# A two-layer hybrid mixer network: norms by token parts between three tiles on either side, and a folded Fourier mixer

## The chip, the cores and the metric

The kernel runs on one core of one Trainium2 chip. Its engines work at the same time and wait for one another by semaphores: TensorE (PE, matrix products), VectorE (DVE), ScalarE (ACT), GpSimd (POOL) and SyncE (SP, which only issues transfers). The metric is the device time of one execution in microseconds.

## What is computed

Two layers over 512 latent tokens and 256 context tokens, 1024 features each. Each layer normalises, modulates, projects to four groups of mixers, projects back and adds; then the same around a gated feed-forward network (FFN). From the reference, cut:

```python
u = modulate(rms_norm(x, g_pre_mix[l]), sh1, sc1) @ w_in[l]
...
o_b = fourier_mix(ub) @ w_fnet[l]      # real part of a 2-D FFT over tokens and 64 channels
...
mix = jnp.concatenate([merge(o_a), o_b, merge(o_c), o_d], axis=-1) @ w_out[l]
x = x + gt1 * rms_norm(mix, g_post_mix[l])
ffn = swiglu(modulate(rms_norm(x, g_pre_ffn[l]), sh2, sc2), w_ffn_in[l], w_ffn_out[l])
x = x + gt2 * rms_norm(ffn, g_post_ffn[l])
```

The context runs through the same weights in layer 0 with its own modulation. In layer 1 it is only needed for keys, values and states, so most of that layer works on the 512 latent tokens alone. `sh1`, `sc1`, `gt1` and their kind are products of the conditioning vectors with a large matrix.

## The kernel before

Features lie on the 128 partitions in 8 chunks (NC), tokens along the free dimension. The width T is 768 (TOK) in layer 0 and 512 (LAT) in layer 1. A weight tile has 128 output features and up to 8 chunks of contraction. Each is split into a high part (ScalarE, L570) and a low part (VectorE, L1154), the activations too, and one chunk takes three fp32r products: high by high, high by low, low by high (`passes`, L808). At T of 768 each is two products of 384 columns, in two PSUM banks; at 512 it is one. Tiles alternate between `ps[0]` and `ps[1]`.

The weights stream through three slots (RING = 3). SyncE loads tile k when tile k-3 has been multiplied:

```python
sp.wait_ge(blk_done, k - RING + 1)
sp.dma_start(raw[:, k % RING], wstream[tile_source(k)]).then_inc(raw_ld[k % RING], 16)
```

A layer is 22 projection tiles, the attention and recurrence mixers, the Fourier mixer, 8 output tiles ("wout"), and three FFN pieces of 8, 8 and 6 hidden chunks (`FFN_CHUNKS`), each with its "in" tiles and 8 "out" tiles.

Between two phases stands a norm. The post norm needs the squares of all 8 finished tiles: GpSimd squares and adds the first seven (L491, L493), ScalarE squares the last (L713), and TensorE sums over partitions with a matrix of ones in exact f32 (L871). ScalarE makes the inverse root by a logarithm and an exponential (L708, L709). VectorE then scales each chunk (L1248) and adds it to x (L1252). The pre norm squares the new x chunk by chunk (ScalarE L702, TensorE L859), makes a root, and produces the modulated input's high half (ScalarE L723) and low half (VectorE L1226, L1233). The next phase begins with two tiles side by side, which take each chunk as its low half is ready; a third tile's weights are loaded already.

The Fourier mixer multiplies channels with `fn_d` (L883), ScalarE copies (L778), then tokens are multiplied with cosine and sine tables of full width in exact f32 (L891), VectorE copies (L1514), and `fn_w` is applied (L899). The modulation columns of the coming stages are made by "pairs": GpSimd loads two rows (L477) when the reductions before them are done, and VectorE does four reductions over 1024 elements (`ada_pair`, L1166) that write their dump into `ps[3]`. In layer 0 pairs 8 and 9 stand in the Fourier mixer, 10 and 11 among the output tiles, the rest in the FFN.

Every engine takes its instructions in the order written.

## Time and profile before

| | |
|---|---|
| time, median of 3 runs | 1851.71 us (1851.44 to 1854.57) |
| the profiled execution's own time | 1851.98 us |
| its span | 1850.2 us |
| TensorE busy | 1704.0 us |
| VectorE busy | 980.6 us |
| ScalarE busy | 596.2 us |
| GpSimd busy | 149.1 us |
| mean granted TensorE clock | 0.974 of full |

The span runs from the first to the last instruction; the execution's own time has 1.8 us around it. Busy time says how much an engine worked, not whether the end waited for it: for that the profile has a chain, followed back from the last instruction to what released each step.

### The profile page before, as it was taken

The page shows a single profiled execution, that of the slowest core. Times are in us where ns is not written, and L with a number is a line of the kernel's source. Part 1 is how long each engine was busy: PE and PEld are TensorE (multiplying, and loading weights), DVE is VectorE, ACT ScalarE, POOL GpSimd, SP SyncE. Part 2 cuts the span into 40 slices and gives each one's busy share as a digit, 9 for nine tenths or more (in the row PEclk, how much of TensorE's full clock was granted, in tenths as well). Part 3 has the DMA queues.
Part 4 walks back from the last instruction along what each step waited for, and adds up shares of the span by engine and source line. Part 5 has one row for each costly group of instructions (what it writes and reads, how often), then busy time and mean ns, then how long its engine had stood idle before and what let it go on. Part 6 is the DMA issues. An engine that isn't in the chain of part 4 may idle for free.

```text
span 1850.2 us, 24632 instructions
## 1 busy us (share of the span) xinstructions
PE 1704.0 (92%) x10460; PEld 1501.7 (81%) x10460; DVE 980.6 (53%) x1603; ACT 596.2 (32%) x796; POOL 149.1 (8%) x186
## 2 busy tenths in 40 slices
PE   2699998999799999999999979898899899999996
PEld 1699987769599999999999959796667587887874
DVE  7987536865566544555554372653762632233334
ACT  2334433732332222221122143542462422332231
POOL 1010001004100000000000400000103000000003
PEclk9899999999899999999999989999999899999998
DMA  8261124132133334333432202113402132232222
GB/s 335 88 204 48 47 63 105 50 114 84 54 103 116 124 125 135 116 126 125 128 113 91 69 23 69 58 47 83 112 34 69 46 102 91 91 102 91 91 92 102
DMA packets 80638, 178.84 MB, mean 97 GB/s; under 512 B 38912, under 2 KB 39424, under 8 KB 80272
## 3 DMA queue, kind: packets, MB, share of 16 engines
q1 hardware_dynamic: 66864, 122.70, 21.7%
q0 software_dynamic: 13664, 54.56, 8.6%
q8 instruction: 83, 1.36, 0.3%
q14 instruction: 27, 0.22, 0.0%
HBM read 175.14 MB, written 2.10 MB: 96 GB/s over the span
## 4 chain that ended last, share of the span: by engine, by line
PE 85%; DVE 9%; DMA 3%; ACT 2%; issue 1%; SPq 0%; DVEq 0%; ACTq 0%
PE psum L808 73%; PE psum L969 2%; PE psum L980 2%; PE psum L1003 2%; DMA ada_0a<-in_adaT 1%; DVE f_t L1248 1%; PE psum L1034 1%; DVE x L1252 1%; PE psum L859 1%; DVE tmp L1226 1%; PE psum L891 1%; DVE psum L1545 1%; DVE w_lo L1154 1%; DVE psum L1166 1%; DVE s_sb L1324 1%
## 5 line engine op out<-in xcount | busy, mean ns | idle before, releaser
L808 PE MATMUL psum<-h_hi,w_hi 128*128 128x384 f32 (+1 forms) x1872 | 560.4, 359 | 32.1 <-DVE h_lo L1233 27.3
L808 PE MATMUL psum<-h_lo,w_hi 128*128 128x384 f32 (+1 forms) x1872 | 547.5, 352 | 0.0
L808 PE MATMUL psum<-h_hi,w_lo 128*128 128x384 f32 (+1 forms) x1872 | 547.2, 352 | 0.0
L1154 DVE TENSOR_TENSOR w_lo<-raw,w_hi 128x1024 fp32r<-128x1024 f32 x194 | 241.2, 1243 | 352.2 <-ACT w_hi L570 350.9
L808 PEld LDWEIGHTS psum<-h_hi,w_hi 128*128 128x128 f32 x1872 | 342.7, 190 | 61.5 <-issue 34.7
L570 ACT ACTIVATE w_hi<-raw 128x1024 fp32r<-128x1024 f32 x194 | 205.6, 1060 | 501.3 <-DMA raw<-in_wstream 501.2
L808 PEld LDWEIGHTS psum<-h_lo,w_hi 128*128 128x128 f32 x1872 | 346.4, 190 | 20.6 <-issue 1.7
L808 PEld LDWEIGHTS psum<-h_hi,w_lo 128*128 128x128 f32 x1872 | 345.6, 190 | 19.9
L1166 DVE CUSTOM_DVE_ANT_0 psum<-ada_w,c_b 128x1024 f32<-128x1024 f32 x160 | 202.2, 1264 | 16.3 <-issue 3.7
L1194 DVE TENSOR_TENSOR tmp<-tmp,psum 128x768 f32<-128x768 f32 (+1 forms) x44 | 36.1, 821 | 263.6 <-PE psum L808 263.6
L808 PE MATMUL psum<-hid_hi,w_hi 128*128 128x384 f32 (+1 forms) x528 | 160.2, 357 | 15.6 <-DVE w_lo L1154 13.2
L808 PE MATMUL psum<-hid_lo,w_hi 128*128 128x384 f32 (+1 forms) x528 | 159.1, 355 | 0.0
L808 PE MATMUL psum<-hid_hi,w_lo 128*128 128x384 f32 (+1 forms) x528 | 159.0, 355 | 0.0
L808 PEld LDWEIGHTS psum<-hid_hi,w_hi 128*128 128x128 f32 x528 | 97.0, 189 | 27.1 <-DVE w_lo L1154 17.3
L808 PEld LDWEIGHTS psum<-hid_hi,w_lo 128*128 128x128 f32 x528 | 97.7, 190 | 7.0
L808 PEld LDWEIGHTS psum<-hid_lo,w_hi 128*128 128x128 f32 x528 | 97.8, 190 | 6.7
L859 PE MATMUL psum<-sq,consts 128*128 128x512 f32 (+1 forms) x112 | 50.0, 604 | 51.8 <-ACT sq L702 51.7
L477 POOL DMA_DIRECT2D ada_w<-in_adaT x78 | 41.3, 530 | 635.7 <-DVE ada_t L1166 635.1
L859 PEld LDWEIGHTS psum<-sq,consts 128*128 128x128 f32 x112 | 23.8, 226 | 77.5 <-issue 50.2
L491 POOL TENSOR_TENSOR sq<-f_t 128x768 f32<-128x768 f32 (+1 forms) x28 | 41.1, 1467 | 537.5 <-DVE f_t L1181 446.6
L692 ACT ACTIVATE hid_hi<-tmp 128x768 fp32r<-128x768 f32 (+1 forms) x44 | 32.5, 739 | 116.8 <-DVE tmp L1194 116.8
L588 ACT ACTIVATE u_t<-psum 128x768 f32<-128x768 f32 (+1 forms) x44 | 33.6, 763 | 100.7 <-PE psum L808 100.4
(168 smaller groups left out, 1453.9 us busy)
## 6 DMA issues: line engine op xcount, KB each, us to landing
raw<-in_wstream SPq DMA_DIRECT2D x196, 512.0 KB, 3.6
ada_w<-in_adaT POOLq DMA_DIRECT2D x80, 512.0 KB, 4.0
ada_0a<-in_adaT SPq DMA_DIRECT2D x6, 1024.0 KB, 14.3
x<-in_xT POOLq DMA_DIRECT2D x4, 1536.0 KB, 10.9
na_r<-in_rpb SPq DMA_DIRECT2D x64, 64.0 KB, 3.4
fn_l<-in_dftL POOLq DMA_DIRECT2D x2, 2048.0 KB, 8.2
ada_0b<-in_adaT SPq DMA_DIRECT2D x2, 1024.0 KB, 19.3
out_xT<-x SPq DMA_DIRECT2D x4, 512.0 KB, 2.8
```

What stands on the lines that cost most here:

```text
L477: pool.dma_start(ada_w[:, u], adaT[2 * ADA_ORDER[q] + (2 * ADA_FIRST + u)]).then_inc(ada_ld[u], 16)
L491: link(pool.tensor_tensor(sq[:, 1 if b == 0 else 0, 0:T], f, f, ALU.mult))
L570: act.activation(w_hi[:, k % RING].rearrange("p c n -> p (c n)"), raw[:, k % RING], ACT.Copy)\
L588: act.activation(as_product(u_t[:, blk, 0:T], T), product_of(ps[b % 2], T), ACT.Silu if blk >= QD else ACT.Copy).then_inc(bank_free[b % 2], 1)
L808: mm = pe.matmul(ps[u][:, at:at + hi - lo], w[:, slot, k], r[:, k, lo:hi], start=first, stop=last)
L859: mm = pe.matmul(ps[2][:, lo:hi], ones, sq[:, c % 2, lo:hi], start=c == 0, stop=c == NC - 1)
L969: mm = pe.matmul(dst, q, keys, start=True, stop=True)
L980: mm = pe.transpose(pt_ps[:, n * j + P * c:n * j + P * c + P], s_sb[:, v % 3, j, o:o + P], ident)
L1003: mm = pe.matmul(dst, val, pt_sb[:, v % 2, n * j + P * c:n * j + P * c + P], start=c == 0, stop=c == n // P - 1, skip_group_check=True)
L1154: dve.tensor_tensor(w_lo[:, k % RING].rearrange("p c n -> p (c n)"), raw[:, k % RING], w_hi[:, k % RING].rearrange("p c n -> p (c n)").bit ...
L1166: dve.tensor_tensor_reduce(ps[3][:], ada_w[:, u], c_b[:, v], 1.0, 0.0, ALU.mult, ALU.add, ada_t[:, u, v:v + 1]).then_inc(ada_done, 1)
L1194: dve.tensor_tensor(as_product(tmp[:, 1, 0:T], T), as_product(tmp[:, 0, 0:T], T), product_of(ps[1], T), ALU.mult).then_inc(bank_free[1], 1)
```

## The change

1. **Norms by token parts.** The tokens are divided in two: in layer 0 the 256 context tokens (part 0) and the 512 latent ones (part 1), in layer 1 two halves of 256. The last three tiles before a norm (`tail`) are multiplied first for part 0 and then for part 1, and the first three tiles after it (`head`) as well. Each part has its own squares, roots, post and pre norm. TensorE's sums of squares of part 0's new x stand inside the second tail tile, those of part 1's post norm inside the first head tile. The head's part 1 takes all three tiles chunk by chunk; in layer 0's widths it is one product of 384 and one of 128 columns. The third tile of tail and head uses `ps[3]`. The last norm has no pre norm, and its stores go out by part.
2. **Fourier mixer folded.** A cosine table is symmetric and a sine table antisymmetric, so only n/2+1 cosine and n/2-1 sine columns are multiplied. ScalarE copies the sine sums, VectorE adds them to the cosines and subtracts them in reversed order for the other half. The tables are loaded in two transfers each.
3. **Modulation pairs.** In layer 0 pairs 8 and 9 leave the Fourier mixer: output tile pairs 0, 1 and 2 now have pairs (8, 9), 10 and 11. GpSimd loads 9, 10 and 11 each before two of its squares. The FFN's pairs shift by a tile. The third tail tile waits until pair 11 is copied.

```diff
+TAIL, HEAD = 3, 3
+def norm_parts(T):
+    return ((LAT, TOK, 1, 512), (0, LAT, 0, 0)) if T == TOK else ((0, T // 2, 0, 0), (T // 2, T, 0, 512))
...
+            def head_pieces(T, p):
+                if T == TOK:
+                    return ((0, HALF, 0), (HALF, LAT, 512)) if p else ((LAT, TOK, 512 + LAT - HALF),)
+                lo, hi, _, _ = norm_parts(T)[p]
+                return ((lo, hi, lo),)
+            def tail(g0, rhs_hi, rhs_lo, kc, T, nb, pre):
+                parts = norm_parts(T)
+                for p, (lo, hi, _, at0) in enumerate(parts):
+                    for j in range(TAIL):
+                        b = N_OUT - TAIL + j
+                        if p == 0:
+                            pe.wait_ge(w_lo_done, 2 * g0 + b + 1)
+                            if j < 2:
+                                pe.wait_ge(bank_free[b % 2], b // 2 + (g0 + 1))
+                            elif nb < 2:
+                                pe.wait_ge(ada_copied, (13, 41)[nb])
+                        else:
+                            pe.wait_ge(tail_free, TAIL * nb + j + 1)
+                        for k in range(kc):
+                            mm = passes_into(tail_bank(j), 2 * g0 + b, k, rhs_hi, rhs_lo, ((lo, hi, at0),), k == 0, k == kc - 1)
+                            if k == kc - 1:
+                                mm.then_inc(blk_done if p else tail_done, 1)
+                            if p and j == 0 and k == 2:
+                                late_mean_square(parts[0])
+                            if p and j == 1 and pre:
+                                part_mean_square(parts[0], NC * k // kc, NC * (k + 1) // kc)
+            def head(g0, T, nb):
...
+                for j in range(HEAD):
+                    pe.wait_ge(w_lo_done, 2 * g0 + j + 1)
+                    for k in range(NC):
+                        if j == 0:
+                            pe.wait_ge(hlo_ready, base + k + 1)
+                        passes_into(head_bank(j), 2 * g0 + j, k, h_hi, h_lo, head_pieces(T, 0), k == 0, k == NC - 1)
+                        if j == 0 and k == 3:
+                            late_mean_square(parts[1])
+                part_mean_square(parts[1], 0, NC)
+                for u in range(2):
+                    pe.wait_ge(bank_free[u], g0 + 1)
+                for k in range(NC):
+                    pe.wait_ge(hlo_ready, base + NC + k + 1)
+                    for j in range(HEAD):
+                        mm = passes_into(head_bank(j), 2 * g0 + j, k, h_hi, h_lo, head_pieces(T, 1), k == 0, k == NC - 1)
+                        if k == NC - 1:
+                            mm.then_inc(blk_done, 1)
```

The order on ScalarE and on VectorE in one norm (definitions of the steps left out; `copied` is ScalarE's copy of a wout tile, `added` VectorE's add of an FFN tile):

```diff
+                for j in range(TAIL):
+                    copied(0, j)
+                post_root(0)
+                pre_root(0)
+                copied(1, 0)
+                split_hi(2 * (g0 + N_OUT // 2))
+                normed_hi(0, 0, NC // 2)
+                copied(1, 1)
+                normed_hi(0, NC // 2, NC)
+                split_hi(2 * (g0 + N_OUT // 2) + 1)
+                copied(1, 2)
+                post_root(1)
+                split_hi(2 * (g0 + N_OUT // 2) + 2)
+                pre_root(1)
+                normed_hi(1, 0, NC)
...
+                for j in range(TAIL):
+                    added(0, j)
+                root()
+                post(0, 0, NC)
+                dve.wait_ge(x_upd, nx[0])
+                added(1, 0)
+                if pre is None:
+                    added(1, 1)
+                    added(1, 2)
+                    root()
+                    post(1, 0, NC)
+                    dve.wait_ge(x_upd, nx[0])
+                    return
+                root()
+                normed(0, 0, NC // 2)
+                split_lo(nxt)
+                added(1, 1)
+                normed(0, NC // 2, NC)
+                split_lo(nxt + 1)
+                added(1, 2)
+                root()
+                post(1, 0, 2)
+                split_lo(nxt + 2)
+                post(1, 2, NC)
+                dve.wait_ge(x_upd, nx[0])
+                root()
+                normed(1, 0, NC)
```

The Fourier mixer on TensorE and VectorE, the modulation pairs among the output tiles, and GpSimd's order:

```diff
+                    for part in (1, 0):
+                        for lo, n, blocks, z in folded_streams(T):
+                            tab, columns = fn_c if lo else fn_l, (slice(0, n // 2 + 1), slice(n // 2 + 1, n))[part]
+                            at0 = 512 + z + 1 if part else z
+                            dst = ps[b][:, at0:at0 + columns.stop - columns.start]
+                            for j in range(blocks):
+                                mm = pe.matmul(dst, fn_ab[:, lo // P + j, 256 * b + P * part:256 * b + P * part + P],
+                                               tab[:, j, columns], start=j == 0, stop=j == blocks - 1)
+                        mm.then_inc(fn_s if part else fn_t, 1)
...
-                    if l == 0:
-                        ada_pair(8 + b)
...
+                    for lo, n, _, z in st:
+                        cosines = ps[b][:, z:z + n // 2 + 1]
+                        dve.tensor_tensor(fn_f[:, b, lo:lo + n // 2 + 1], cosines, fn_z[b][:, z:z + n // 2 + 1], ALU.add)
+                        ins = dve.tensor_tensor(backwards(fn_f[:, b, lo + n // 2 + 1:lo + n]), cosines[:, 1:n // 2],
+                                                fn_z[b][:, z + 1:z + n // 2], ALU.subtract)
+                    ins.then_inc(fn_te, 1)
...
-                        split_lo(2 * tp["wout"] + 2 * i + u + 2)
-                    if l == 0 and i < 2:
-                        ada_pair(10 + i)
+                        if 2 * i + u <= N_OUT - TAIL:
+                            split_lo(2 * tp["wout"] + 2 * i + u + 2)
+                    for q in ((8, 9), (10,), (11,), ())[i] if l == 0 else ():
+                        ada_pair(q)
...
-                    ada_loads(11, 1)
-                    squares(tp["wout"], 0, N_OUT, T)
+                    for i in range(3):
+                        ada_loads(9 + i, 1)
+                        squares(tp["wout"], 2 * i, 2, T)
+                    tail_squares(tp["wout"], T, 2 * l)
```

## Rows read from the trace of the kernel before

**Rows 1.** The page: busy time and chain.
```profile
PE 1704.0 (92%) x10460; PEld 1501.7 (81%) x10460; DVE 980.6 (53%) x1603; ACT 596.2 (32%) x796; POOL 149.1 (8%) x186
...
PE 85%; DVE 9%; DMA 3%; ACT 2%; issue 1%; SPq 0%; DVEq 0%; ACTq 0%
```

**Rows 2.** Chain in order of time: start, duration, engine, tile and line, count.
```profile
410.42 66.77 PE psum L808 x384
...
506.23 135.10 PE psum L808 x768
...
1031.44 37.69 PE psum L808 x216
...
1098.31 63.69 PE psum L808 x336
...
1407.27 32.94 PE psum L808 x144
...
1460.70 12.79 PE psum L808 x48
...
1702.62 92.76 PE psum L808 x408
...
1812.03 20.66 PE psum L808 x90
```

**Rows 3.** Timeline of TensorE in layer 0's Fourier mixer.
```profile
394.41 7.03 PE L891 MATMUL psum<-fn_l,fn_ab 128*128 128x512 f32 x16
...
401.28 1.89 PE L891 MATMUL psum<-fn_c,fn_ab 128*128 128x256 f32 x8
```

**Rows 4.** Timeline around a slot's turn: SyncE, ScalarE, VectorE.
```profile
1062.91 6.57 SPq L429 DMA_DIRECT2D raw<-in_wstream  x2
...
1066.60 1.06 ACT L570 ACTIVATE w_hi<-raw 128x1024 fp32r<-128x1024 f32 x1 [5.34 <-DMA raw<-in_wstream]
...
1067.69 1.22 DVE L1154 TENSOR_TENSOR w_lo<-raw,w_hi 128x1024 fp32r<-128x1024 f32 x1 [3.82 <-ACT w_hi L570]
```

**Rows 5.** Timeline of a root at the end: square, exponential, first scaling.
```profile
1833.50 0.63 ACT L713 ACTIVATE lnms<-f_t 128x512 f32<-128x512 f32 x1 [8.48 <-DVE f_t L1181]
...
1836.06 0.63 ACT L709 ACTIVATE rstd<-lnms 128x512 f32<-128x512 f32 x1
...
1836.79 1.42 DVE L1248 SCALAR_TENSOR_TENSOR f_t<-f_t,col_gg,rstd 128x512 f32<-128x512 f32 x2 [3.10 <-ACT rstd L709]
```

**Rows 6.** Chain in order of time, a post norm's chunk at 768 tokens.
```profile
485.56 1.06 DVE f_t L1248 x2
486.62 0.87 DVE x L1252
```

**Rows 7.** Groups by form: exact f32 products of 128 columns; weight loads.
```profile
L1082 PE MATMUL psum<-hv,hk 128*128 128x128 f32 x80 | 10.2, 275 | 0.0
...
L1003 PEld LDWEIGHTS psum<-pt_sb,sw_v 128*64 128x64 f32 x352 | 18.8, 136 | 3.7 <-issue 3.0 <-ACT pt_sb L738 0.7
...
L1082 PEld LDWEIGHTS psum<-hv,hk 128*128 128x128 f32 x80 | 10.1, 191 | 0.2
```

**Rows 8.** Timeline of the end: GpSimd, VectorE, stores.
```profile
1827.29 1.04 POOL L491 TENSOR_TENSOR sq<-f_t 128x512 f32<-128x512 f32 x1 [1.82 <-DVE f_t L1181]
...
1845.71 1.29 DVE L1252 TENSOR_TENSOR x<-x,f_t 128x512 f32<-128x512 f32 x2
...
1840.10 7.30 SPq L467 DMA_DIRECT2D out_xT<-x  x4
```

**Rows 9.** The page: group of the reductions; issues of their loads.
```profile
L1166 DVE CUSTOM_DVE_ANT_0 psum<-ada_w,c_b 128x1024 f32<-128x1024 f32 x160 | 202.2, 1264 | 16.3 <-issue 3.7
...
ada_w<-in_adaT POOLq DMA_DIRECT2D x80, 512.0 KB, 4.0
```

**Rows 10.** Timeline of VectorE, a reduction while GpSimd squares.
```profile
442.45 2.87 DVE L1166 CUSTOM_DVE_ANT_0 psum<-ada_w,c_b 128x1024 f32<-128x1024 f32 x1
```

**Rows 11.** Windows: length, busy time and count by engine, granted clock, DMA.
```profile
506.00:510.00 4.00, 3.77 (x13) 3.80 (x14) 3.93 (x8) 1.97 (x4) 0.00 (x0) 0.57 0.00 0
```

More of the change, by code:

```diff
@@ L573, in copy_phase @@
             def copy_phase(g0, n, dst, b0, T):
-                for b in range(2 * n):
+                for b in range(n):
                     k = 2 * g0 + b
@@ L802, in passes, with passes_into @@
             def passes(tile, k, rhs_hi, rhs_lo, T, begin, end):
-                u, slot = tile % 2, tile % RING
+                return passes_into(ps[tile % 2], tile, k, rhs_hi, rhs_lo, pieces(T), begin, end)
+            def passes_into(bank, tile, k, rhs_hi, rhs_lo, tokens, begin, end):
+                slot = tile % RING
                 for w, r, first, last in ((w_hi, rhs_hi, begin, False), (w_hi, rhs_lo, False, False),
                                           (w_lo, rhs_hi, False, end)):
-                    for lo, hi, at in pieces(T):
-                        mm = pe.matmul(ps[u][:, at:at + hi - lo], w[:, slot, k], r[:, k, lo:hi], start=first, stop=last)
@@ L822, in side_by_side, with product_phase @@
                             mm.then_inc(blk_done, 1)
-            def product_phase(g0, n, rhs_hi, rhs_lo, kc, T, ready=None, order=range(NC)):
+            def product_phase(g0, n, rhs_hi, rhs_lo, kc, T, ready=None, order=range(NC), first=0):
                 if ready:
                     side_by_side(g0, rhs_hi, rhs_lo, kc, T, ready, order[:kc])
-                for b in range(2 if ready else 0, 2 * n):
+                for b in range(2 if ready else first, n):
                     pe.wait_ge(w_lo_done, 2 * g0 + b + 1)
@@ L1176, in lo_phase @@
                         k = 2 * (g0 + i) + u
+                        if 2 * i + u > 2 * n - tail:
+                            continue
                         split_lo(k + 2)
[L1178 removed]
+                        if add and 2 * i + u < 2 * n - tail:
                             dve.wait_ge(blk_done, k + 1)
```

313 lines of the change are left out of this document (217 added, 96 removed).

## The prediction

> **What bounds the kernel now.** I read the page's busy table and its chain first: TensorE is busy 1704.0 of 1850.2 us and holds 85% of the chain, VectorE 9% [rows 1]. So the change must shorten TensorE's pauses or its work. The chain in order of time gives the pace and the pauses [rows 2]: full-width products run back to back (37.69 us for 216 products of 384 columns, 0.174 us each; 92.76 us for 408 of 512 columns, 0.227 us), and the chain leaves TensorE for 29.2 us between 477.2 and 506.2, as long between 1069.1 and 1098.3, for 20.5 us between 1440.2 and 1460.7, and for 17.5 us from 1832.7 to the end. These are the four norm boundaries B1 to B4. A straight line through the two paces is columns/2.4 GHz plus 14 ns: 0.121 us for 256 columns.
>
> Two other views set the prices. An exact f32 product is recorded twice: 16 records of 512 columns take 7.0 us and 8 of 256 take 1.9, so a sum of squares over 512 tokens (two records) costs 0.88 us and one over 256 tokens 0.47 us [rows 3]. And the ring of three weight slots has a fixed turn-round: a tile's products end at 1062.7, its load is issued, its high half starts at 1066.6 and its low half ends at 1068.9, 6.2 us after the slot came free [rows 4].
>
> **Boundary B1, step by step.** t is counted from the first product of the sixth output tile. Before: three tiles 25.0, pause 29.2, first three FFN tiles 26.7 (25.0 plus the 1.7 by which the 768 products from 506.2 on exceed their pace): 80.9.
>
> After, part 0 (256 tokens) of three tiles costs 2.9 each; the third waits for its weights until 6.2, so it ends at 9.2. Copy and square (0.4 each, where 512 elements take 0.63), two sums of squares (0.93), logarithm and exponential (1.0) and the hand-overs that [rows 5] show bring the first root to VectorE at 13.3. The post norm of a chunk costs 0.40 for the scaled product (the pair of 512 and 256 takes 1.06, and 512 alone 0.66) and 0.34 for the add (768 take 0.87, and 512 half of 1.2) [rows 5, 6, 8], eight chunks end at 19.7. But TensorE carries the eight sums of squares inside the second tile's part 1: 9.2+5.5+0.9, then 5.5+3.7, to 24.8. VectorE has the pre-norm root at 26.0; it idles 6 us. ScalarE then stands before it with a tile copy (0.6) and a weight split (1.06), so the first low half ends at 28.5; at 0.92 a chunk and with a weight split between (1.2), the head may start at 32.7. TensorE was done at 30.2.
>
> The head is queued behind another wait: after four chunks of its first tile (34.2) it holds the squares' sum of part 1, and that square is behind four more chunks on VectorE, a split on ScalarE and VectorE and the third tile's copy: 38.7. Whatever else the head has is behind that. The second root reaches VectorE at 41.4, two chunks and a split end at 45.1, the remaining six at 52.8. TensorE does the third head tile until 48.1 and then eight sums of 512, with two buffers 0.93 apart, to 55.5. Root 57.3, first low half 59.6. Part 1 of three tiles is 72 pairs of 384+128 columns.
>
> **The unseen size: 128 columns.** No such product of this kind is in the trace. From below the line gives 0.067; the exact f32 product of 128 columns takes 0.128 a record (10.2 us for 80) and 0.255 for its two [rows 7]. The weight load lengthens from 136 to 191 ns between 64 and 128 columns, 54 ns for 64, so a load should need about 0.108 and cannot hide behind 53 ns of columns. I take 0.124, near the record; the ends go into the range. With it part 1 costs 8x9x0.298=21.5, and B1 ends at 81.1: +0.2. With the ends it is -3.9 or +9.6. The Trainium skill ("TensorE: Matmul & The Clock Gate", LDWEIGHTS) gives a load as columns over 1.2 GHz, 107 ns for 128, with which the 144 such products would cost 2.4 us less than with 0.124; its isolated gap (Back-to-back issue gap), 56 ns, would take off 9.8 us. The rows' 54 ns for 64 columns agrees with the first.
>
> **The other boundaries**, by the same steps. B2 (six chunks of contraction, VectorE adds instead of ScalarE's copy): part 0 ends 8.5, first root 12.8, squares 21.3, head 28.7, second root 39.2, part 1 from 57.4 to 78.9; before 18.8+29.2+26.7=74.7: +4.2. B3 (512 tokens, halves of 256): squares end 20.2, head 27.8, second root 35.2, part 1 from 48.2 to 56.9; before 16.4+20.5+18.3 (12.8 for the two that start together, 5.5)=55.2: +1.7. B4 (end): part 0 ends 8.5, VectorE has the root at 12.2 and the first post norm to 18.6; only then does it add the three part-1 tiles (19.7); GpSimd's squares of two tiles (1.04 and 1.3 a tile at 512, about 1.3 at 256) end 21.7, root 23.9, last add 30.3, store 2.7 more, as it now ends 3.2 after the last add [rows 8]: 33.0 against 29.9, +3.1. Sum of the four: +9.2.
>
> **The fourth tile.** The head ends its three tiles together: the first tile frees its slot only 1.8 us before the end (0.7 in B3). The load of the fourth cannot start before, and takes the 6.2 of [rows 4]. Before, two tiles shared the start and the third lay ready as cover of 8.3 (5.5 in B3). So TensorE stands 4.4, 4.4 and 5.4 us: +14.2.
>
> **The Fourier mixer.** Folding leaves the number of products and halves their columns, 512 to 257 and 255, context alike. Layer 0: 17.4 us of products become 9.4; VectorE's copy (0.95) becomes adds and subtracts of 1.3, without the 0.8 for which the modulation pair held it; the sine copy on ScalarE (0.8) is hidden behind the 2.3 us of cosines. -8.4. Layer 1: 32 records of 512, 14.0 [rows 3], become 7.4 and the copy grows 0.1: -6.5. Table loads are halved and lay early before; nothing.
>
> **The moved modulation pairs.** A pair is four reductions with their reads, 5.3 us. A reduction's mean is 1.26, and its weights' load lands 4.0 after issue [rows 9]. With everything 8.4 earlier, VectorE splits the fourth output tile's weights until 423.6, then does pairs 8 and 9 before the fifth tile's weights. Pair 9's loads are queued on GpSimd behind pair 8: pair 9 ends at 436.2 alone. While GpSimd squares, a reduction takes 2.3 to 2.9 [rows 10]: then 438.8. TensorE wants the fifth tile at 435.1 and gets it at 437.4 to 440.3. Then the eighth tile's part 0 waits for pair 11, which VectorE starts only after that tile's weight split: 5.4 more, up to 6.3. Together 7.5 to 11.4; I take 9.4. So layer 0's Fourier and output stretch comes to +1.0: the folding is paid back there.
>
> **Two further prices.** When TensorE resumes after B1's pause, the granted clock is mostly at its lower level of 1.2 GHz: 0.57 of full in 506 to 510 [rows 11]; that is the 1.7 above. Before has one in each boundary, in my sum already; the new order pauses before part 1 and before the fourth tile. I add one to each of B1 to B3: +5.1; two is the bound. GpSimd's squares of part 1 now fall into VectorE's pre norm. The rows' doubled time over some 5 us would cost 2.5, none is the other end; I take 1.5 three times: +4.5. The Trainium skill ("GPSIMD Engine Reference", its table's SBUF interfaces) states that the port is shared with VectorE's instructions of two SBUF inputs; the trace agrees, and by the rule alone the norm's scaled products would all be slowed.
>
> **Sum.** 1.0 + 9.2 + 14.2 - 6.5 + 5.1 + 4.5 = +27.5. The profiled span of 1850.2 becomes 1877.7; 1.8 lie around it, and the median shown is 0.3 under the profiled execution's own 1852.0: 1879.
>
> **Rivals.** (a) A 128-column product costs as the doubled f32 one: 18.7 more over B1 and B2, 1898. For it: nothing here runs below 384 in this form. 0.15. (b) The light case: 0.067, no further low clock, no port loss: 1879-8.2-9.6, 1861. Against: load length and clock rows. 0.17. (c) The fourth tile isn't late, because the load or the splits turn round in the last chunk's time: 1879-14-5, 1860. Against: [rows 4], whose 6.2 us recur at every slot. 0.10. (d) Faster, by one mechanism: the norm passes keep ahead of TensorE. My timetable holds TensorE 13, 17 and 12 us in B1 to B3 for VectorE and ScalarE; if chunk passes and roots of part 0 finished before TensorE's squares and copies, these 42 us would go: 1837. It decides from 9 us a boundary. For it: VectorE is busy only 53% overall [rows 1]. Against: inside a boundary VectorE has 30 us of work in two passes, with four roots in series where there were two, and 256 elements cost VectorE 0.40 where 512 cost 0.66 [rows 6]. 0.13. My forecast keeps 0.45.
>
> Range: 1853 to 1900 takes in (a), (b), (c) and the bounds of the pairs; it leaves out (d) and a little above. A difference of 0.2% (3.7 us) is what the measurement can tell. Faster 0.12, mostly (d); same 0.08, the low edge of (b) and (c); slower 0.80.
>
> **What the profile after would show.** TensorE's fourth tile after each head should start about 6 us after the first head tile's end, released by the low weight half. In the first head tile a pause of some 4 us after four chunks, released by a square. Pairs of 384+128 at 0.298. L891's products at half their time. In layer 0's output stretch, pauses before the fifth and eighth tile released by w_lo and the modulation copy. Last add 30 us after the tail's start. I would be wrong if VectorE's idle in B1 to B3 is small and TensorE's too, above all if the fourth tile follows without pause.

## The result, and the profile after

| | before | changed |
|---|---|---|
| time, median | 1851.59 us (1851.44 to 1854.57, 4 runs) | 1910.9 us (1909.86 to 1911.78, 4 runs) |
| ratio, 95% interval | | 1.0306 [1.0287, 1.0326] |
| profiled span | 1850.2 us | 1910.0 us |
| mean granted clock | 0.974 | 0.958 |

The change makes the kernel 59 us slower. The forecast was slower by 27; the time lies above its range. The page of the changed kernel, first its busy times, then the chain by engine, against [rows 1]:

```profile
PE 1722.9 (90%) x10826; PEld 1536.4 (80%) x10826; DVE 999.0 (52%) x1697; ACT 608.8 (32%) x858; POOL 161.2 (8%) x206
...
PE 81%; DVE 9%; DMA 5%; ACT 3%; issue 1%; POOL 0%; SPq 0%; DVEq 0%; POOLq 0%; ACTq 0%
```

TensorE's busy time is 18.9 us longer although the Fourier products are halved, and its share of the chain fell from 85 to 81%: most of the 60 us are pauses. The chain in order of time (start, length, what) says where, next to [rows 2]:

```profile
448.34 11.23 PE psum L931 x48
532.20 20.70 PE psum L931 x132
559.04 110.40 PE psum L931 x624
671.76 201.71 PE psum L931 x1152
1139.75 20.70 PE psum L931 x132
1166.55 38.15 PE psum L931 x192
1500.44 9.39 PE psum L931 x60
1531.51 73.17 PE psum L931 x312
```

Before, 768 products stood in one piece from 506.23, and 216 began at 1031.44. Now the head's part 1 is a piece of its own (20.70 us in B1 and B2), then the chain leaves TensorE for 6.1 us, and then comes the fourth tile.

Phase by phase, after less before, from the start times of the product at which the same sum of columns has been multiplied in the two traces. The forecast's prices for clock (1.7) and port (1.5) stand in each of B1 to B3, as its own text puts them, and so do the waits of the fourth tile. The eighth tile's wait for pair 11 stands with the output tiles, less the 0.4 us that B1's timetable has for it:

| stretch | forecast | measured |
|---|---|---|
| layer 0 up to the first output tile (Fourier; 1.0 of it inside the mixer) | -8.4 | -1.3 |
| output tiles of layer 0 (modulation pairs) | +9.4 | +17.9 |
| B1, B2, B3, B4 | +7.8, +11.8, +10.3, +3.1 | +9.4, +10.9, +10.2, +3.8 |
| products behind the fourth tile (FFN twice, projections) | 0 | +3.7, +3.7, +2.3 |
| Fourier mixer of layer 1 | -6.5 | -0.7 |
| sum | +27.5 | +59.8 |

So the four boundaries, where most of the working went, came out at 34.3 against 33.0. Of the miss of 32.3 us, 12.9 lie in the two Fourier mixers, 8.5 in the output tiles, and 9.6 in full-width products behind the boundaries.

**The Fourier mixer of layer 0.** ScalarE's timeline of the changed kernel (start, length, engine, line, operation, count; in brackets the idle time ahead and what ended it), then VectorE's, then TensorE's:

```profile
387.92 0.55 ACT L901 ACTIVATE fn_z<-psum 128x255 f32<-128x255 f32 x2 [2.52 <-PE psum L1085]
392.26 0.55 ACT L901 ACTIVATE fn_z<-psum 128x255 f32<-128x255 f32 x2 [3.79 <-PE psum L1085]
392.70 4.50 ACT L905 ACTIVATE h_hi<-f_t 128x768 fp32r<-128x768 f32 x6
```

```profile
393.58 5.30 DVE L1851 TENSOR_TENSOR h_lo<-f_t,h_hi 128x768 fp32r<-128x768 f32 x6 [13.90 <-ACT h_hi L905]
399.04 0.43 DVE L1788 TENSOR_TENSOR fn_f<-psum,fn_z 128x257 f32<-128x257 f32 x1
...
400.97 0.28 DVE L1789 TENSOR_TENSOR fn_f<-psum,fn_z 128x127 f32<-128x127 f32 x1
```

```profile
389.90 1.89 PE L1085 MATMUL psum<-fn_l,fn_ab 128*128 128x255 f32 x8
...
392.06 1.90 PE L1085 MATMUL psum<-fn_l,fn_ab 128*128 128x257 f32 x8
...
401.30 7.87 PE L1092 MATMUL psum<-fn_f,fn_w 128*128 128x512 f32 x16 [6.89 <-DVE fn_f L1789]
```

L1085 has two groups of 1.9 us where L891 had one of 7.0 [rows 3]: that term is right. But ScalarE has the two sine copies written ahead of the six high halves of `h`. Before, it made those halves while TensorE multiplied. Now it waits for the second sine sums until 392.3; VectorE stands 13.9 us for the first high half, and its six low halves (5.3) are written ahead of the fold. TensorE, done at 394.4, gets `fn_f` at 401.3, and then runs its 16 products at the lower clock, 7.87 us instead of some 5.4. The products are gained and the time is spent in two queues.

**The output tiles of layer 0.** TensorE's pauses there, then the pieces of the chain that lead to the second:

```profile
448.34 1.01 PE L931 MATMUL psum<-h_hi,w_hi 128*128 128x384 f32 x2 [5.67 <-DVE w_lo L1349]
475.02 0.55 PE L931 MATMUL psum<-h_hi,w_hi 128*128 128x256 f32 x1 [9.72 <-DVE ada_c L1365]
```

```profile
459.58 6.25 DMA raw<-in_wstream
465.86 1.06 ACT w_hi L626
...
468.09 1.64 DVE psum L1361
...
474.71 0.18 DVE ada_c L1365
```

Both pauses stand where the prediction put them. The first is 5.67 us, above its bound of 5.2, and the 48 products behind it take 11.23 us in the chain where their pace gives 8.35: 2.9 more at the lower clock, which the forecast did not have here. The second is nearly twice its 5.4. The load of the eighth tile takes 6.25, so its weight split ends 8.5 us after the slot came free at 459.6 and not 6.2. Only at 468.1 does VectorE start pair 11, and its reductions beside GpSimd's squares take 6.8.

**The boundaries.** TensorE's pauses in B1 and, last two rows, the fourth tile of B2 and of B3:

```profile
502.92 0.38 PE L931 MATMUL psum<-h_hi,w_hi 128*128 128x256 f32 x1 [2.64 <-DVE w_lo L1349]
505.28 1.13 PE L1053 MATMUL psum<-sq,consts 128*128 128x512 f32 x2 [0.68 <-POOLq L544]
510.04 2.08 PE L1053 MATMUL psum<-lnms,consts 128*128 128x512 f32 x2 [3.63 <-ACT lnms L800]
532.20 0.47 PE L931 MATMUL psum<-h_hi,w_hi 128*128 128x384 f32 x2 [3.93 <-DVE h_lo L1483]
559.04 1.01 PE L931 MATMUL psum<-h_hi,w_hi 128*128 128x384 f32 x2 [4.44 <-DVE w_lo L1349]
...
1166.55 1.01 PE L931 MATMUL psum<-h_hi,w_hi 128*128 128x384 f32 x2 [4.39 <-DVE w_lo L1349]
...
1531.51 0.80 PE L931 MATMUL psum<-h_hi,w_hi 128*128 128x512 f32 x1 [5.40 <-DVE w_lo L1349]
```

4.44, 4.39 and 5.40 us for the fourth tile: the prediction said 4.4, 4.4 and 5.4. It is the trace's turn-round of a weight slot [rows 4]: 6.1 us from the end of the chain's piece to the fourth tile. Behind it the clock is at its lower level again, in windows of TensorE's time (length, busy, count, granted clock, DMA share, GB/s):

```profile
559.00:561.00 2.00, 1.96 (x6) 0.50 0.08 33
561.00:563.00 2.00, 2.00 (x8) 0.50 0.00 0
563.00:567.00 4.00, 4.00 (x24) 0.97 0.00 0
```

The 12 products of 384 columns that start in this stretch take 4.0 us for 2.1, and it is much the same in B2 and B3: 5.9 of the 9.6 us behind the boundaries. Most of the rest are two places further on, each behind a pause of 2.1 to 2.3 us that the kernel before has too. There the clock now falls (0.62 of full in 672 to 674) where it did not before (1.00 in 644 to 646), and the same products take 1.6 us longer, before and then after:

```profile
643.66 200.16 PE psum L808 x1152
...
1552.11 11.16 PE psum L808 x48
```

```profile
671.76 201.71 PE psum L931 x1152
...
1606.73 12.76 PE psum L931 x48
```

### The profile page after: what moved, and what is told of

It is laid out like the page before. It is cut to its first block, busy times and chain, and to the rows that moved or that the text cites. A ratio compares the mean times of both kernels' runs of the same rounds, so it can differ in the third digit from the quotient of the medians.

```text
span 1910.0 us, 25588 instructions
## 1 busy us (share of the span) xinstructions
PE 1722.9 (90%) x10826; PEld 1536.4 (80%) x10826; DVE 999.0 (52%) x1697; ACT 608.8 (32%) x858; POOL 161.2 (8%) x206
## 4 chain that ended last, share of the span: by engine, by line
PE 81%; DVE 9%; DMA 5%; ACT 3%; issue 1%; POOL 0%; SPq 0%; DVEq 0%; POOLq 0%; ACTq 0%
PE psum L931 68%; DMA raw<-in_wstream 2%; PE psum L1162 2%; PE psum L1173 2%; PE psum L1196 2%; PE psum L1062 2%; DVE w_lo L1349 1%; DMA ada_0a<-in_adaT 1%; PE psum L1227 1%; ACT w_hi L626 1%; DVE psum L1361 1%; DVE tmp L1477 1%; PE psum L1092 1%; DVE psum L1822 1%; DVE s_sb L1589 1%
## 5 line engine op out<-in xcount | busy, mean ns | idle before, releaser
L931 PE MATMUL psum<-h_hi,w_hi 128*128 128x384 f32 (+3 forms) x1968 | 595.4, 357 | 67.4 <-DVE w_lo L1349 35.3
L931 PE MATMUL psum<-h_lo,w_hi 128*128 128x384 f32 (+3 forms) x1968 | 576.5, 347 | 0.0
L931 PE MATMUL psum<-h_hi,w_lo 128*128 128x384 f32 (+3 forms) x1968 | 575.7, 347 | 0.0
L931 PEld LDWEIGHTS psum<-h_hi,w_hi 128*128 128x128 f32 x1968 | 364.3, 194 | 99.5 <-issue 40.4
L1361 DVE CUSTOM_DVE_ANT_0 psum<-ada_w,c_b 128x1024 f32<-128x1024 f32 x160 | 204.7, 1279 | 19.6 <-DMA ada_w<-in_adaT 10.5
L931 PE MATMUL psum<-hid_hi,w_hi 128*128 128x384 f32 (+2 forms) x546 | 169.2, 357 | 18.8 <-DVE w_lo L1349 16.1
L931 PE MATMUL psum<-hid_hi,w_lo 128*128 128x384 f32 (+2 forms) x546 | 166.6, 352 | 0.0
L931 PE MATMUL psum<-hid_lo,w_hi 128*128 128x384 f32 (+2 forms) x546 | 166.6, 352 | 0.0
L523 POOL TENSOR_TENSOR sq<-f_t 128x512 f32<-128x512 f32 (+2 forms) x36 | 43.4, 1206 | 573.4 <-DVE f_t L1378 422.7
L746 ACT ACTIVATE tmp<-psum 128x768 f32<-128x768 f32 (+1 forms) x44 | 31.1, 706 | 99.4 <-PE psum L931 99.4
L868 ACT ACTIVATE s_sb<-s_sb,nb 128x512 f32<-128x512 f32 (+3 forms) x80 | 56.8, 713 | 7.8 <-DVE nb L1593 6.5
## 6 DMA issues: line engine op xcount, KB each, us to landing
x<-in_xT POOLq DMA_DIRECT2D x4, 1536.0 KB, 10.9
```

What stands on the lines that cost most here:

```text
L523: link(pool.tensor_tensor(sq[:, 1 if b == 0 else 0, lo:hi], f, f, ALU.mult))
L868: act.activation(p, p, ACT.Exp, bias=nb[:, s % 3, j:j + 1], scale=SCALE, accum_out=sums[:, s % 3, j:j + 1]).then_inc(at_p, 1)
L931: mm = pe.matmul(bank[:, at:at + hi - lo], w[:, slot, k], r[:, k, lo:hi], start=first, stop=last)
L1361: dve.tensor_tensor_reduce(ps[3][:], ada_w[:, u], c_b[:, v], 1.0, 0.0, ALU.mult, ALU.add, ada_t[:, u, v:v + 1]).then_inc(ada_done, 1)
```

## The experiments

"Three fixes" below are the edits of the first three experiments together. The kernel before ran beside each group, with medians of 1851.9 to 1853.2.

**1. High halves first.** The changed kernel, with the sine copies moved down ScalarE's order:

```diff
-                for b in range(2):
-                    act.wait_ge(fn_s, 2 * l + b + 1)
...
                 for n, c in enumerate(MIX_ORDER):
+                    if n == NC - 2:
+                        for b in range(2):
+                            act.wait_ge(fn_s, 2 * l + b + 1)
...
                     act.wait_ge(mix_done, MIXERS * l + (2 if n < NC - 2 else 3))
```

> The changed kernel, but ScalarE makes the six high halves of the mixed activations (4.5 us) before the two copies of the sine sums; nothing else. Theory: in the changed kernel the second sine copy waits for TensorE until 392.3, so the six high halves stand behind it, VectorE's six low halves end at 398.8 instead of 391.7, the fold stands behind these, and the next products start at 401.3 after a 6.9 us pause and at the lower clock (7.9 us instead of 5.1). Then this order gives back 7.5 us in layer 0 and 5.5 in layer 1: 1898 us (changed kernel 1910.9). Rival: the output stretch of layer 0 absorbs its share, because the pairs there run by their own loads and not by TensorE's start: only layer 1's 5.5, 1905. Second rival: the folded products themselves are slow: no change.

1894.15 us, ratio 1.0219 [1.0202, 1.0236]: 16.8 less than the changed kernel. In TensorE's timeline of this kernel the pause ahead of the `fn_w` products is 1.24 where it was 6.89, and they run in 5.43 where they took 7.87:

```profile
396.43 5.43 PE L1093 MATMUL psum<-fn_f,fn_w 128*128 128x512 f32 x16 [1.24 <-DVE fn_f L1790]
```

From `fn_d` to the first output tile this kernel is 9.1 us shorter than the kernel before, and layer 1's mixer is 6.8 shorter; the forecast had 8.4 and 6.5. So the order of one engine's queue cost all that the folding was to bring, and the lower clock behind the pause came with it.

**2. Pairs earlier.** Pairs 8 and 9 ahead of the fourth output tile's weight split; 10 and 11 keep their place.

```diff
-                    for q in ((8, 9), (10,), (11,), ())[i] if l == 0 else ():
-                        ada_pair(q)
+                        for q in ((8, 9) if u == 0 else (), (10,) if u else (), (11,) if u else (), ())[i] if l == 0 else ():
+                            ada_pair(q)
```

> The changed kernel, but VectorE does modulation pairs 8 and 9 before the fourth output tile's weight split instead of after it, where it idles 15.8 us for that weight. Theory: the 5.7 us wait for the fifth tile's weights (and the lower clock after it, about 1 us) go; pair 10's loads are issued earlier too, so pair 11 ends earlier against the eighth tile: in all 9 to 15 us less, 1896 to 1902. Rival: the eighth tile's wait for pair 11 (9.7 us) only grows by what the fifth tile's wait loses, as pair 11 is bound to GpSimd's squares and loads: within 2 us of 1910.9.

1904.34 us, 1.0283 [1.0267, 1.0299], 6.6 less, neither the 9 to 15 of the theory nor the nothing of the rival. The fifth tile's pause is gone, and the stretch up to the sixth tile is 8.6 us shorter. The eighth tile's pause stays (9.10 us, released by the modulation copy).

**3. A head of two tiles.** The third tile's weight split stays where the head had it.

```diff
-TAIL, HEAD = 3, 3
+TAIL, HEAD = 3, 2
...
-            return ps[3] if j == HEAD - 1 else ps[j % 2]
+            return ps[j % 2]
```

> The changed kernel with two tiles in the head instead of three (HEAD 2; the third tile is multiplied at full width after them, its weights are split where they were). Theory: the pauses before the fourth tile (5, 4.4 and 5.4 us) go, since the third tile gives 8.3 or 5.5 us of cover as in the kernel before, with some 2 us each of lower clock after them, and 24 fewer 128-column products in two places take 1.5 us each: 18 to 24 us less, 1887 to 1893. Rival: the pauses come from something else than the ring's turn-round (the exit of the norm on VectorE or ScalarE) and move behind the third tile: within 5 us of 1910.9.

1885.44 us, 1.0188 [1.0164, 1.0213]: 25.5 less. Its chain in order of time, B1 and then B3:

```profile
529.11 16.32 PE psum L931 x96
545.56 116.77 PE psum L931 x672
664.68 200.13 PE psum L931 x1152
...
1501.59 76.46 PE psum L931 x336
```

No pause stands between head and third or fourth tile. But the three waits (14.2) do not come back whole: by stages of the two profiles B1, B2 and B3 are 3.3, 3.2 and 5.3 us shorter. In B1 the third tile takes 8.3 us at full width where its 24 pairs took 6.9, and part 1 starts only 1.3 us sooner though 2.9 us of products went from ahead of it. The greater part of the gain, 6.8, 3.0 and 3.8 us, lies in the products behind the boundaries. The three restarts at the lower clock are gone (5.9), and so are four falls of the clock behind pauses of 2.1 to 2.3 us (6.3 together); one of them, in the changed kernel and then here:

```profile
875.80 18.48 PE psum L931 x96
```

```profile
867.14 16.88 PE psum L931 x96
```

Whether these four belong to the edit, one profile each does not show.

**4. The norms alone.** The changed kernel, with the Fourier mixer and the pairs of the kernel before.

```diff
-                    for q in ((8, 9), (10,), (11,), ())[i] if l == 0 else ():
+                    for q in ((10,), (11,), (), ())[i] if l == 0 else ():
...
+                    if l == 0:
+                        ada_pair(8 + b)
                     dve.wait_ge(fn_t, 2 * l + b + 1)
-                    dve.wait_ge(fn_sc, 4 * l + len(st) * (b + 1))
...
+                    dve.tensor_copy(fn_f[:, b, 0:T], ps[b][:, 0:T]).then_inc(fn_te, 1)
```

> The changed kernel's norms by parts with the Fourier mixer and the modulation pairs of the kernel before. Theory: the norms carry their own cost, by the ledger of the two traces 9.1 + 11.8 + 10.3 + 3.7 at the four boundaries and about 8 of lower clock in the phases behind them: 1851.6 + 43 = 1894. Rival: the norms are near neutral and the loss is the pairs' and the Fourier mixer's: under 1870.

1896.54 us, 1.0235 [1.0215, 1.0254], +44.6: the norms carry three quarters of the loss.

**5. Fold and pairs alone.** The other half of the change on the kernel before, norms whole: `folded_tables`, the sine copies and `fourier` as changed, and

```diff
-                    if l == 0 and i < 2:
-                        ada_pair(10 + i)
+                    for q in ((8, 9), (10,), (11,), ())[i] if l == 0 else ():
+                        ada_pair(q)
```

> The kernel before with the changed kernel's Fourier mixer and modulation pairs, norms left whole. The norms alone gave +44.6 over before and the whole change +59.3. If the two halves add, this kernel is at +14.7, 1866.6 us: the slow order on ScalarE and the pairs' waits (two pauses of some 5 and 9 us in layer 0's output stretch, the second only where the eighth tile uses the bank that the reductions write, which whole norms don't do). My theory is that the eighth tile's pause goes with the whole norms, so that this kernel is some 8 us under the sum: 1858, and the rest is an interaction of the two parts. Rival 1: they add plainly, 1866. Rival 2: fold and pairs alone are faster than before, as their removed work says: under 1848.

1859.57 us, 1.003 [1.0012, 1.0048], +7.1. The halves sum to +51.7, and the whole is +59.3: some 8 us exist only together. Each of the three differences has an interval of 3 to 4 us on either side, so this sum alone would be weak; experiments 9 and 12 bear on it again. This kernel has the fifth tile's pause (4.82 us) and none at the eighth.

**6. Three fixes at once.** The diffs of 1, 2 and 3 together.

> The changed kernel with three edits at once: ScalarE's six high halves ahead of the sine copies, pairs 8 and 9 ahead of the fourth output tile's weight split with 10 and 11 after later splits, and a head of two tiles in place of three. If the three causes are separate, their single gains add: 1910.9 - 16.8 - 6.6 - 25.5 = 1862. Rival: they share waits (what one gives, the next takes back), 1872 to 1885. Either way above the kernel before's 1852, since two passes of VectorE in each boundary and the eighth tile's wait for pair 11 are left: a result under 1848 would say that the norms by parts pay once their head is short.

1867.91 us, 1.008 [1.0059, 1.0101]. The single gains sum to 48.9, together they give 43.0: 6 us under the sum. Some 3 of it may be the clock: this profile has two such falls, that of kernel 3 none. Norms by parts do not pay with a short head either.

**7. The fold repaired.** Whole norms, the fold with ScalarE's order of experiment 1, pairs 8 and 9 after the third tile's split, 10 after the sixth's, 11 after the eighth's.

```diff
                         split_lo(2 * tp["wout"] + 2 * i + u + 2)
-                    if l == 0 and i < 2:
-                        ada_pair(10 + i)
+                        for q in (((8, 9), ()), ((), (10,)), ((), (11,)), ((), ()))[i][u] if l == 0 else ():
+                            ada_pair(q)
```

> The kernel before with whole norms, the folded mixer with ScalarE's six high halves ahead of the sine copies, pairs 8 and 9 after the third output tile's weight split, 10 after the sixth's and 11 after the eighth's. If the fold's loss was only its queue order and the pairs' place, both gains come through: 8.4 in layer 0 and 6.5 in layer 1, 1837, at most 1842 if a weight split is still late behind a pair. Rival: the pairs cost in the output stretch whatever their place (VectorE's reductions slowed by GpSimd's squares, loads in competition with the weight stream): 1846 to 1852.

1836.07 us, 0.9899 [0.9881, 0.9917]: 16 us faster than the kernel before. The output tiles stand in the chain as one piece again, 66.77 us as in [rows 2], 9.8 us earlier:

```profile
400.62 66.77 PE psum L826 x384
496.43 135.19 PE psum L826 x768
```

**8. The fold, pairs where they were.** Kernel 7, with

```diff
+                    if l == 0:
+                        ada_pair(8 + b)
                     if b == 0:
                         for z in range(4):
...
-                        for q in (((8, 9), ()), ((), (10,)), ((), (11,)), ((), ()))[i][u] if l == 0 else ():
+                        for q in (((), (10,)), ((), (11,)), ((), ()), ((), ()))[i][u] if l == 0 else ():
```

> As the repaired fold, but with the modulation pairs where the kernel before has them, 8 and 9 inside the Fourier mixer. Theory: in layer 0 VectorE's two pairs, 5.3 us each, set the end of the mixer, so the halved products gain nothing there and the adds cost 0.4 more than the copies; only layer 1 gains, 6.5: 1845.8. Then the difference to the repaired fold is what moving the pairs is worth, some 8. Rival: the pairs fit into other idle time of VectorE and layer 0 gains as well: 1838 to 1840, level with the repaired fold.

1845.52 us, 0.996 [0.9945, 0.9974]. GpSimd's loads of the pairs are back too. TensorE's timeline of this kernel says why layer 0 gains nothing:

```profile
385.68 1.99 PE L911 MATMUL psum<-fn_l,fn_ab 128*128 128x255 f32 x8 [0.69 <-ACT fn_ab L789]
...
405.13 1.22 PE L918 MATMUL psum<-fn_f,fn_w 128*128 128x512 f32 x1 [10.49 <-DVE fn_f L1544]
```

With its products halved TensorE waits 10.5 us for VectorE's two pairs, and its `fn_w` products start when they started before (405.0 then). They run at the lower clock behind the wait and take 7.22 us where they took 5.43, so this mixer is 2.0 us longer than before; layer 1's is 6.8 shorter. Moving the pairs was necessary, and worth 9.4.

**9. A tail of two tiles.** Kernel 6, with the weight splits where they were, and

```diff
-TAIL, HEAD = 3, 2
+TAIL, HEAD = 2, 2
...
-            return ps[(1, 0, 3)[j]]
+            return ps[j]
```

> The kernel with three fixes, and the tail cut from three tiles to two as well (they use the two ordinary banks, so the eighth tile no longer waits for pair 11). The kernel with three fixes has 8.8 us of such a pause. My theory: VectorE's passes set the end of a boundary, and they start with part 0's end; that comes 3.3 us sooner in the first boundary and some 2 later in each of the other three, because the sixth tile is now multiplied whole before it: about +2.5, 1870. Rival 1: the pause is on the path whole: 1867.9 - 8.8 = 1859. Rival 2: a two-tile tail gives TensorE 5.5 us less to do under VectorE's passes in each boundary and each of these shows: 1880 or more.

1860.04 us, 1.0033 [1.002, 1.0047]. My theory (1870) fell, the first rival holds: 7.9 less, nearly the whole 8.77 us that the eighth tile waited for pair 11 in kernel 6, and by stages 8.1 of it lies in B1. This is what the two halves of the change cost together.

**10 and 11. Third split last; late square after.** Kernel 6 with the first of these edits (and `split_hi` likewise), and kernel 6 with the second:

```diff
-                split_lo(nxt + 2)
                 post(1, 2, NC)
                 dve.wait_ge(x_upd, nx[0])
                 root()
                 normed(1, 0, NC)
+                split_lo(nxt + 2)
```

```diff
-                        if j == 0 and k == 3:
+                        if j == 0 and k == NC - 1:
                             late_mean_square(parts[1])
```

> The kernel with three fixes, and in each boundary the third tile's weight split (1.2 us on VectorE, 1.06 on ScalarE) taken from between the norm passes to behind them; the third tile is wanted only 16 us later. If the passes of VectorE set the end of a boundary, three times 1.2 goes: 1864.3, or 1861 where ScalarE's 1.06 stands on the same path. Rival: the passes wait for roots and squares at that point, so a split fits in for nothing: 1867.9 within 1.5.

> The kernel with three fixes, and TensorE's sums of squares of part 1 moved from the middle of the head's first tile to its end. In that kernel TensorE stands 3.3 us in the middle of the tile, waiting for that square. Theory: TensorE's pause there is not on the path, VectorE and ScalarE produce the square at the same time in either order: 1867.9 within 1.5. Rival: the 1.5 us of products that now come under the pause are won in each of three boundaries: 1863.5.

1867.44 (1.008 [1.0063, 1.0097]) and 1867.87 us (1.008 [1.0065, 1.0095]): neither is told from 1867.91. For the late square that is the theory: TensorE's 3.3 us pause there costs nothing, since VectorE and ScalarE produce the square. For the split it is less clear. The profiled kernel 10 is 1.8 us shorter than kernel 6 in B1, as the theory had it, but B2 is as long and B3 is 0.5 longer, and the piece of 1152 behind B1 is 201.53 long, where kernel 6 has 200.16. So the split was on the path in one boundary at most.

**12. Norms alone, short head.** Kernel 4 with the diff of 3.

> Norms by parts alone (Fourier mixer and pairs as before), with a head of two tiles in place of three. Norms alone gave +44.6, and the short head took 25.5 off the whole change: 1871, +19 over before, if the head's loss is a thing of the norms alone. The kernel with three fixes stands 31.8 over the repaired fold with whole norms; the difference, 12.7, would then be what norms by parts and the moved pairs cost together, above all the eighth tile's wait for pair 11. Rival: no such interaction, then this kernel is at 1851.9 + 31.8 = 1884.

1878.1 us, 1.0132 [1.0117, 1.0147], +24.9: between theory and rival. The short head is worth 18.4 here and 25.5 in the whole change. By the profiles the two gains are 19.8 and 28.2, and 4.7 of these 8.4 us are the clock behind those short pauses: four falls became none there, and four became three here. The rest I can't place. The whole change with the short head stands 31.8 over kernel 7 (experiment 6), the norms alone with it 24.9 over the kernel before: 6.9 us again exist only together.

**13 to 15. What is left.** Kernel 9 stands 24 us over kernel 7. By phases of their traces that is +7.0 in B1, +6.5 in B2, +6.6 in B3, +3.0 at the end, and 2.1 before the output tiles. The two "further prices" of the prediction were tried: GpSimd's square of part 1 left out (13, on kernel 9; its sum of squares then lacks that tile, so it is no kernel to keep), and 16 products with unused results put into TensorE's last pause of a boundary, in whole norms (14, on kernel 7) and in norms by parts (15, on kernel 9):

```diff
                             pool.wait_ge(bank_free[b % 2], g0 + b // 2 + 2)
-                        square(b, lo, hi)
+                        if p == 0:
+                            square(b, lo, hi)
```

```diff
+            def keep_busy(slot, n=16):
+                for _ in range(n):
+                    pe.matmul(ps[3][:, 0:512], w_hi[:, slot, 0], w_hi[:, slot, 0:4].rearrange("p c n -> p (c n)"),
+                              start=True, stop=True)
...
+                keep_busy(2 * g0 % RING)
                 for k in range(NC):
                     pe.wait_ge(hlo_ready, base + NC + k + 1)
```

> The kernel with two-tile head and tail, in which GpSimd leaves out its square of the tail tile for part 1 (one square and one add for each norm; the sum of squares lacks that tile). If GpSimd's work slows VectorE's pre norm of part 0 or the square is late for TensorE, its removal gains up to the forecast's 1.5 us in each of three boundaries, and something at the end, where the root waits for it: 1860.0 - 4.5 - 1 = 1854.5. My theory after reading the traces: with one tile less in the tail the squares fall under VectorE's work at two instructions only (2.6 us in place of 0.9, seen once in a boundary), and that is on the path: 1.7 for each of three, 1855. Rival: VectorE has idle time behind it, 1860 within 1.5.

> The kernel with two-tile head and tail, with 16 extra products of 512 columns in the 3.9 us pause ahead of the head's part 1 in three boundaries. Theory: the restart at the lower clock goes there (0.59 of full in its first 4 us), 1.3 to 1.7 each: 1860.0 - 4.5 = 1855.5. If also nothing else of the boundary moves, some 15 of the 24 us over whole norms then belong to the passes of VectorE and ScalarE themselves. Rival: 1860 within 1.5, because the head's part 1 is paced by VectorE's chunks (1.5 us each against 1.25 of products for two tiles) and not by TensorE.

> The kernel with whole norms and the repaired fold, with 16 extra products of 512 columns in the pause of TensorE ahead of the first two tiles after each of three norms (results unused). The pauses are 5.3, some 5 and 3.9 us, 16 products take 3.6. Theory: the granted clock stays at its upper level through them and the 1.7 us lost in each restart come back: 1836.1 - 5.1 = 1831. Rival: the clock falls during norm or dummies all the same, or the extra products end late: 1836 within 1.5 or above.

Kernel 13: 1856.67 us, 1.0017 [1.0006, 1.0029], 3.4 less. By stages of the two profiles that is 1.3 in B1, 0.1 in B2, 0.2 in B3 and 1.5 at the end, where the last root no longer waits for the square; 1.6 more lie ahead of the output tiles, where the edit changed nothing. Where VectorE's scaled product of 256 elements took 1.36 us beside GpSimd (first row, kernel 9), it takes 0.48 (second row, kernel 13):

```profile
477.54 1.36 DVE L1476 SCALAR_TENSOR_TENSOR tmp<-x,col_gs,rstd 128x256 f32<-128x256 f32 x1
```

```profile
475.95 0.48 DVE L1477 SCALAR_TENSOR_TENSOR tmp<-x,col_gs,rstd 128x256 f32<-128x256 f32 x1
```

Kernel 15: 1854.49 us, 1.0002 [0.999, 1.0013], 5.5 less; the theory had 4.5, the prediction 5.1. By stages it is 2.2 in B1, 2.7 in B2 and 0.2 in B3. The granted clock of 508 to 512, in TensorE's windows of kernel 9 and then of kernel 15:

```profile
508.00:512.00 4.00, 3.69 (x15) 0.59 0.01 4
```

```profile
508.00:512.00 4.00, 4.00 (x31) 1.00 0.00 0
```

Kernel 14: 1834.44 us, 0.9893 [0.9877, 0.9909], not told from kernel 7's 1836.07. Its three restarts are shorter, 134.59 us for 768 products against 135.19, 62.31 against 63.68 and 11.73 against 12.77, 3.0 in all; but two pieces elsewhere are longer, 201.71 against 200.16 and 12.67 against 11.16. So the restarts cost 0.6 to 1.4 each there, less than the 1.7 that the theory took, and the rest was lost at other pauses.

## Why the prediction was wrong in size

**Right.** The sign, and by mechanism nearly all of the boundaries: the fourth tile's wait to a tenth of a microsecond, the pause for the late square in the head (3.63 us, some 4 forecast), nearly the pair of 384 and 128 columns (0.298 taken; at a granted clock of 1.00 pairs start 0.287 apart from 536 us on, so the narrow product costs 0.113 and not 0.124), the halved Fourier products, both pauses among the output tiles. Rival (d), the norm passes keeping ahead of TensorE, is not what the runs show: even with short head and tail (kernel 9 against 7) each boundary costs 3 to 7 us more than with whole norms.

That the boundaries' sum is so close is in part luck. In B1 part 1 starts 63.5 us into the timetable (the pair's 9.3 taken off), where 59.6 and the port's 1.5 give 61.1, and then takes 22.4 us, where 21.5 and the restart's 1.7 give 23.2. B2's stretch before is 75.7 us and not 74.7: the prediction took B1's 1.7 us for its restart, which cost 2.6 there. And between 477.2 and 506.2 lie 29.0 us, not 29.2.

**The step that failed first** is "The Fourier mixer": "the sine copy on ScalarE (0.8) is hidden behind the 2.3 us of cosines". It asked what covers the copy and not what is queued behind it. Behind it stood six high halves of 4.5 us and, on VectorE, six low halves of 5.3 ahead of the fold, work that lay under TensorE's products before. Experiment 1 gives the price, 16.8 us over the two layers, against a forecast gain of 14.9 of which 1.7 arrived inside the mixers.

**The second** is a term that was mis-sized: the moved pairs, 9.4, with bounds of 7.5 to 11.4. They measured 17.9. The wait for pair 11 was taken from its own 5.4 us, as if the weight split ahead of it were on time. The split was 2.3 us late (6.25 for its load), the pair took 6.8, and the pause was 9.72. At the fifth tile the pause was 5.67, where some 4 was taken, and its restart at the lower clock (2.9) was in no sum. That this wait exists only with the tail's third tile, experiments 5 and 9 show; it stands in the prediction's own list of edits.

**The third** is the clock. The prediction gave one restart more for each of B1 to B3, inside them. Experiment 15 measures 2.2 and 2.7 us for it in B1 and B2, but 0.2 in B3: there the chain's restart is in the head's first tile (9.39 us for 60 products of 256 columns), ahead of the place that the experiment keeps busy. The fourth tile's pause has a restart of its own (0.50 of full for 4 us, above), which the prediction named as the bound ("two is the bound") and left out of the sum. It and its like are 5.9 of the 9.6 us in the products behind the boundaries, and 3.1 are the two falls behind pauses of 2.1 and 2.3 us, which no term has.

**GpSimd's port**: forecast 4.5, 1.5 in each of B1 to B3. Kernel 13 gives 3.4 with one square left out in a two-tile tail, but only 1.3 of it shows in B1 and 0.3 in B2 and B3 together; the end's 1.5 is a wait for the square, not a slower VectorE. The whole change has two such squares and no run isolates them, so that B2 and B3 come out near their forecast does not confirm this price. In B1 one of VectorE's scaled products of 256 elements takes 1.40 us beside them and two more take 2.68, where one takes 0.48 with GpSimd at rest. The Trainium skill ("GPSIMD Engine Reference", its table's SBUF interfaces) states that GpSimd's port is shared with VectorE's instructions of two SBUF inputs; the trace agrees for these, though most of the norm's products meet no square of GpSimd and keep their 0.48.

**What stays open.** If the gains of kernels 13 and 15 add, which no run tried, about 15 us of the 24 between kernels 9 and 7 are left. My reading is that they are the work itself, four roots in series in place of two and twice the number of VectorE's norm instructions at 0.48 for 256 elements where 512 take 0.75; that was argued, not isolated.

## What to carry to other kernels

Folding or shrinking one engine's work moves the end only if the two or three instructions that now come last stand at the head of their queues: when an edit inserts a wait into an in-order engine, list what is queued behind it, and give that work its old place (here one moved loop was worth 17 us). Cutting a norm in parts for overlap multiplies the fixed pieces, roots, hand-overs and narrow instructions, and needs every slot ahead of it free: tiles that finish together leave the next weight load a full turn-round late. The version to keep has whole norms, the fold and the pairs moved, at 0.9899 of the time before.

## What the hardware showed that was not expected

A pause of TensorE of 2.3 us, between the last "in" tile and the first "out" tile, was followed by the lower clock in one kernel's profile and not in another's. TensorE's windows at the same place in kernel 14 and then in kernel 7, whose code there is the same:

```profile
635.00:637.00 2.00, 2.00 (x7) 0.50 0.00 0
```

```profile
635.00:637.00 2.00, 2.00 (x13) 1.00 0.00 0
```

Each such fall costs about 1.5 us (201.71 against 200.16 for the same 1152 products). In the 17 profiles of this case this piece takes 200.1 to 200.2 us eight times and 201.5 to 201.8 nine times, with nothing between. Executions of one kernel differ in step with it: kernel 15's twelve spans run from 1847.7 us at a mean granted clock of 0.978 to 1856.0 at 0.972. A saving of 1 or 2 us read from a single profile may be this and nothing else.
